# A ring of four weight slots, the low part written over the raw slot, and FFN loops unrolled by four

## What is computed

```python
def swiglu(h, w_gate, w_up, w_down):
    return (jax.nn.silu(h @ w_gate) * (h @ w_up)) @ w_down      # 1024 x 2816, 1024 x 2816, 2816 x 1024

x = x + 0.5 * swiglu(rms_norm(x, g[0]), ffn_w_gate[i, 0], ffn_w_up[i, 0], ffn_w_down[i, 0])
```

## Time and profile before

| | |
|---|---|
| median of 3 runs | 1438.19 us (1437.47 to 1438.66) |
| the profiled execution | 1436.46 us |
| its span (first to last instruction) | 1434.7 us |
| mean granted TensorE clock | 0.964 of full speed |
| HBM read | 231.58 MB |
| FFN stages on PE, first to last weight product | about 188 us each, five of them |

### The profile page before, as it was taken

One profiled execution on the slowest core, in us unless ns is written; L12 is line 12 of the kernel. 1 busy time (PEld: TensorE's weight loads), 2 busy tenths in 40 slices (PEclk: granted clock), 3 DMA queues, 4 the chain that ended last, 5 costly groups with the idle time before them and its releaser, 6 DMA issues.

```text
span 1434.7 us, 17436 instructions
## 1 busy us (share of the span) xinstructions
PE 1364.7 (95%) x6616; PEld 1129.3 (79%) x6616; DVE 794.6 (55%) x844; ACT 643.0 (45%) x722; POOL 72.0 (5%) x172
## 2 busy tenths in 40 slices
PE   6999998999999998999999899999998999999997
PEld 5888887867888876788887667888876986788885
DVE  4554469535545456554546755554556875555543
ACT  5434456324443435534345644434345543544342
POOL 2000012000000001000001200000001200000000
PEclk9999999889999999999999989999999996999999
DMA  8555544413655554455554303655553540466560
GB/s 257 192 188 179 201 162 141 153 59 118 206 191 189 183 215 151 145 178 197 183 188 135 117 30 118 221 189 179 201 198 118 170 171 30 138 202 199 179 198 37
DMA packets 158699, 233.29 MB, mean 163 GB/s; under 512 B 7496, under 2 KB 124894, under 8 KB 158654
## 3 DMA queue, kind: packets, MB, share of 16 engines
q1 hardware_dynamic: 156004, 229.19, 48.1%
q10 hardware_dynamic: 2170, 2.68, 0.6%
q0 software_dynamic: 480, 0.80, 0.3%
HBM read 231.58 MB, written 1.05 MB: 162 GB/s over the span
## 4 chain that ended last, share of the span: by engine, by line
PE 87%; DVE 7%; ACT 3%; DMA 1%; issue 1%; POOL 1%; SPq 0%; POOLq 0%; ACTq 0%; DVEq 0%
PE ps L230 25%; PE ps L232 25%; PE ps L231 25%; DVE wl L202 2%; PE ps L1117 2%; PE ps L469 2%; PE ps L311 1%; ACT wh L197 1%; PE ps L822 1%; DMA arena<-in_p 1%; PE ps L246 1%; PE ps L248 1%; PE ps L247 1%; DVE htl L344 1%; DVE x_rows L411 1%
## 5 line engine op out<-in xcount | busy, mean ns | idle before, releaser
L230 PE MATMUL ps<-wl,hth 128*128 128x512 f32 (+2 forms) x1274 | 506.8, 398 | 20.2 <-DVE htl L344 13.8
L232 PE MATMUL ps<-wh,htl 128*128 128x512 f32 (+2 forms) x1274 | 498.9, 392 | 0.0
L231 PE MATMUL ps<-wh,hth 128*128 128x512 f32 (+2 forms) x1274 | 498.7, 391 | 0.0
L600 DVE TENSOR_TENSOR wl<-raw,wh 128x2048 fp32r<-128x2048 f32 x120 | 275.1, 2293 | 204.8 <-ACT wh L556 204.8
L230 PEld LDWEIGHTS ps<-wl,hth 128*128 128x128 f32 x1274 | 243.5, 191 | 71.7 <-issue 13.9
L202 DVE TENSOR_TENSOR wl<-raw,wh 128x2048 fp32r<-128x2048 f32 (+2 forms) x99 | 222.1, 2256 | 139.6 <-ACT wh L197 139.6
L556 ACT ACTIVATE wh<-raw 128x2048 fp32r<-128x2048 f32 x120 | 229.6, 1914 | 123.7 <-PE ps L232 123.7
L232 PEld LDWEIGHTS ps<-wh,htl 128*128 128x128 f32 x1274 | 243.0, 191 | 51.1
L231 PEld LDWEIGHTS ps<-wh,hth 128*128 128x128 f32 x1274 | 243.8, 191 | 47.7
L197 ACT ACTIVATE wh<-raw 128x2048 fp32r<-128x2048 f32 (+2 forms) x99 | 184.3, 1871 | 100.6 <-PE ps L232 81.2
L230 PE MATMUL ps<-wl,prod_h 128*128 128x512 f32 x416 | 162.6, 391 | 0.0
(11 more groups left out here) (307 smaller groups left out, 938.1 us busy)
## 6 DMA issues: line engine op xcount, KB each, us to landing
raw<-in_ffn_w_gate SPq DMA_DIRECT2D x88, 512.0 KB, 4.0
raw<-in_ffn_w_up SPq DMA_DIRECT2D x88, 512.0 KB, 4.9
raw<-in_ffn_w_down SPq DMA_DIRECT2D x88, 512.0 KB, 3.9
raw<-in_w_gate_up SPq DMA_DIRECT2D x44, 512.0 KB, 4.7
raw<-in_even_w_in SPq DMA_DIRECT2D x24, 512.0 KB, 4.6
raw<-in_w_down SPq DMA_DIRECT2D x22, 512.0 KB, 3.9
raw<-in_ple_w_gate SPq DMA_DIRECT2D x16, 512.0 KB, 4.2
raw<-in_w_in SPq DMA_DIRECT2D x16, 512.0 KB, 4.5
```

Of the source, the lines that this page charges most:

```text
L230: nc.tensor.matmul(o, xh, b, start=first, stop=False)
L231: nc.tensor.matmul(o, xh, a, start=False, stop=False)
L232: return nc.tensor.matmul(o, xl, a, start=False, stop=last)
L600: nc.vector.tensor_tensor(wl[:, r, :], raw[:, r, :], wh[:, r, :].bitcast(f32), ALU.subtract)\
```

## The change

`raw` is allocated, given free at once, and `wl` is allocated in its place, so that both names stand for the same bytes: DVE writes the low part over the raw slot. The three rings have four buffers each. SP loads slot m once PE is done with slot m-4 (`weights_used`), where before it waited for the split of slot m-3. ACT's wait for PE ahead of a split becomes that for slot m-4. `Ahead.before` reaches one slot further, and the places in the FFN get `+ LEAD` (1), so every place now splits slot m+1 where it split slot m. The FFN loops have two iterations of four chunks on each of the four engines, with the first two chunks of SP's loop written out. `even_pe` waits for the DVE step `decayed` ahead of turning `e_last`, which no wait covered any longer.

The diff, cut to its core (DVE's and ACT's functions change in the same way):

```diff
-    RING = 3
+    RING = 4
+    LEAD = RING - 3
+    UNROLL = 4
...
-        raw = sb("raw", [P, RING, SLOT])
+        with nc.sbuf_tensor("raw", [P, RING, SLOT], f32) as raw:
+            pass
+        wl = sb("wl", [P, RING, SLOT], f32r)
         wh = sb("wh", [P, RING, SLOT], f32r)
-        wl = sb("wl", [P, RING, SLOT], f32r)
...
         def load_slot(sp, n, pieces):
             if n >= RING:
-                sp.wait_ge(split_ready, n - RING + 1)
+                sp.wait_ge(weights_used, n - RING + 1)
...
-            with sp.Fori(0, NCH - 1) as i:
+            for i in range(2):
                 for j in range(3):
...
+            with sp.Fori(0, (NCH - 3) // UNROLL) as it:
+                for i in range(2, 2 + UNROLL):
+                    for j in range(3):
+                        m = n + 2 + 3 * i + j
+                        sp.wait_ge(weights_used, it * (3 * UNROLL) + (m - RING + 1))
+                        pieces = gate_up(m, j, it * (UNROLL * HC) + (i + 1) * HC) if j < 2 else down(m, it * (2 * UNROLL) + 2 * i)
+                        for dst, src in pieces:
+                            sp.dma_start(dst, src).then_inc(raw_loaded[m % RING], 16)
...
-            with pe.Fori(2, NCH - 1) as c:
-                chunk(c, False)
+            with pe.Fori(0, (NCH - 3) // UNROLL) as it:
+                for c in range(2, 2 + UNROLL):
+                    chunk(it, c)
...
             norm_act(act, s, FFN_GAIN[f], FFN_BANKS)
-            act_ahead.through(act, n + 3)
+            act_ahead.through(act, n + 3 + LEAD)
             rms(act, s)
...
+            with act.Fori(0, (NCH - 3) // UNROLL) as it:
+                for c in range(2, 2 + UNROLL):
+                    split(it, n + 3 * c + 1 + LEAD)
+                    split(it, n + 3 * c + 2 + LEAD)
+                    silu(c, it=it)
+                    split(it, n + 3 * c + 3 + LEAD)
+                    high(c, it=it)
             act_ahead.n += 3 * (NCH - 3)
-            act_ahead.through(act, n + FFN_SLOTS - 1)
-            silu(n + 3 * (NCH - 1) + 1)
-            act_ahead.through(act, n + FFN_SLOTS)
+            act_ahead.through(act, n + FFN_SLOTS - 1 + LEAD)
+            silu(NCH - 1)
+            act_ahead.through(act, n + FFN_SLOTS + LEAD)
             high(NCH - 1, to=last_h)
...
             pe.wait_ge(EV_ACT.sem, EV_ACT.after("w_cols"))
+            pe.wait_ge(EV_DVE.sem, EV_DVE.after("decayed"))
```

More of the change, by code:

```diff
@@ L432, in ffn_load @@
                 load_slot(sp, n + j, gate_up(n + j, j, 0))
-            with sp.Fori(0, NCH - 1) as i:
+            for i in range(2):
                 for j in range(3):
[L436 to L439, removed]
+                    load_slot(sp, n + 2 + 3 * i + j, gate_up(n + 2 + 3 * i + j, j, i * HC + HC) if j < 2 else down(n + 4 + 3 * i, i * 2))
+            with sp.Fori(0, (NCH - 3) // UNROLL) as it:
[6 more added lines that the diff above has]
+                            sp.dma_start(dst, src).then_inc(raw_loaded[m % RING], 16)
             load_slot(sp, n + FFN_SLOTS - 1, down(n + FFN_SLOTS - 1, 2 * (NCH - 1)))
@@ L470, in turn_product, with chunk @@
                 m.then_inc(prod_turned, 1)
-            def chunk(c, first):
+            def chunk(it, c):
                 for half in range(2):
-                    pe.wait_ge(split_ready, c * 3 + (n + half))
+                    m = n + 3 * c - 1 + half
+                    pe.wait_ge(split_ready, it * (3 * UNROLL) + (m + 1))
                     for kk in range(4):
[L477 to L483, removed]
+                        gate_up(m, 4 * half + kk)
+                pe.wait_ge(prod_low, it * UNROLL + (c + f * NCH))
+                pe.wait_ge(split_ready, it * (3 * UNROLL) + (n + 3 * c + 2))
+                down(n + 3 * c + 1, False, False)
+                pe.wait_ge(prod_ready, it * UNROLL + (c + f * NCH + 1))
                 turn_product()
@@ L538, in ffn_act, with silu, high @@
         def ffn_act(act, n, s, f):
-            def silu(used, b=0):
-                act.wait_ge(weights_used, used)
+            def silu(c, b=0, it=0):
+                act.wait_ge(weights_used, it * (3 * UNROLL) + (n + 3 * c + (1 if c else 2)))
                 for tt in range(TT):
                     nc.scalar.activation(silu_g[:, tt, :], ps[:, b + tt, 0:HC], ACT.Silu, scale=rstd[:, tt:tt + 1]).then_inc(silu_ready, 1)
-            def high(c, b=2, to=prod_h):
-                act.wait_ge(prod_turned, c + (f * NCH + 1))
+            def high(c, b=2, to=prod_h, it=0):
+                act.wait_ge(prod_turned, it * UNROLL + (c + f * NCH + 1))
@@ L548, in high, with split @@
                 nc.scalar.activation(to[:, :, :], bank(b).rearrange("p (k t) -> p k t", k=2), ACT.Copy)\
                   .then_inc(prod_high, 1)
[L551 to L556, removed]
+            def split(it, m):
+                act.wait_ge(raw_loaded[m % RING], it * (32 * 3 * UNROLL // RING) + 32 * (m // RING + 1))
+                act.wait_ge(weights_used, it * (3 * UNROLL) + (m - RING + 1))
+                nc.scalar.activation(wh[:, m % RING, :], raw[:, m % RING, :], ACT.Copy).then_inc(high_ready, 1)
@@ L558, in ffn_act @@
             norm_act(act, s, FFN_GAIN[f], FFN_BANKS)
-            act_ahead.through(act, n + 3)
+            act_ahead.through(act, n + 3 + LEAD)
             rms(act, s)
-            silu(n + 2)
-            act_ahead.through(act, n + 4)
+            silu(0)
+            act_ahead.through(act, n + 4 + LEAD)
             high(0, 0)
-            act_ahead.through(act, n + 5)
-            silu(n + 4, 2)
-            act_ahead.through(act, n + 6)
+            act_ahead.through(act, n + 5 + LEAD)
+            silu(1, 2)
@@ L567, in ffn_act @@
+            act_ahead.through(act, n + 6 + LEAD)
             high(1)
[L568 to L573, removed]
+            with act.Fori(0, (NCH - 3) // UNROLL) as it:
[5 more added lines that the diff above has]
+                    high(c, it=it)
@@ L581, in ffn_dve, with multiply @@
         def ffn_dve(dve, n, s, f):
-            def multiply(c, b=0):
+            def multiply(c, b=0, it=0):
                 for tt in range(TT):
-                    dve.wait_ge(silu_ready, c * TT + (f * NCH * TT + tt + 1))
+                    dve.wait_ge(silu_ready, it * (TT * UNROLL) + (c * TT + f * NCH * TT + tt + 1))
                     m = nc.vector.scalar_tensor_tensor(out=prod[:, tt, :], in0=ps[:, b + tt, HC:2 * HC], scalar=rstd[:, tt:tt + 1],
@@ L588, in multiply, with low, split @@
                 m.then_inc(prod_ready, 1)
-            def low(c, b=2, to=prod_l, high=prod_h):
-                dve.wait_ge(prod_high, c + (f * NCH + 1))
+            def low(c, b=2, to=prod_l, high=prod_h, it=0):
+                dve.wait_ge(prod_high, it * UNROLL + (c + f * NCH + 1))
                 nc.vector.tensor_tensor(to[:, :, :], bank(b).rearrange("p (k t) -> p k t", k=2),
                                         high[:, :, :].bitcast(f32), ALU.subtract).then_inc(prod_low, 1)
[L596 to L600, removed]
+            def split(it, m):
+                dve.wait_ge(high_ready, it * (3 * UNROLL) + (m + 1))
+                nc.vector.tensor_tensor(wl[:, m % RING, :], raw[:, m % RING, :], wh[:, m % RING, :].bitcast(f32), ALU.subtract)\
@@ L601, in split @@
                   .then_inc(split_ready, 1)
             norm_dve(dve, s, FFN_GAIN[f], FFN_BANKS)
-            dve_ahead.through(dve, n + 3)
+            dve_ahead.through(dve, n + 3 + LEAD)
             multiply(0)
-            dve_ahead.through(dve, n + 4)
+            dve_ahead.through(dve, n + 4 + LEAD)
             low(0, 0)
-            dve_ahead.through(dve, n + 5)
+            dve_ahead.through(dve, n + 5 + LEAD)
             multiply(1, 2)
-            dve_ahead.through(dve, n + 6)
+            dve_ahead.through(dve, n + 6 + LEAD)
@@ L611, in ffn_dve @@
             low(1)
[L612 to L617, removed]
+            with dve.Fori(0, (NCH - 3) // UNROLL) as it:
+                for c in range(2, 2 + UNROLL):
+                    split(it, n + 3 * c + 1 + LEAD)
+                    split(it, n + 3 * c + 2 + LEAD)
+                    multiply(c, it=it)
+                    split(it, n + 3 * c + 3 + LEAD)
+                    low(c, it=it)
@@ L618, in ffn_dve @@
             dve_ahead.n += 3 * (NCH - 3)
-            dve_ahead.through(dve, n + FFN_SLOTS - 1)
+            dve_ahead.through(dve, n + FFN_SLOTS - 1 + LEAD)
             multiply(NCH - 1)
-            dve_ahead.through(dve, n + FFN_SLOTS)
+            dve_ahead.through(dve, n + FFN_SLOTS + LEAD)
             low(NCH - 1, to=last_l, high=last_h)
```

## The result

| | before | after |
|---|---|---|
| median, each of 6 runs | 1438.43 us (1437.24 to 1439.69) | 1515.75 us (1501.99 to 1532.49) |
| ratio after/before | | 1.051, 95% interval 1.0466 to 1.0554 |
| profiled execution, span | 1436.46, 1434.7 us | 1513.93, 1512.2 us |

What follows compares the result with a forecast made beforehand. PE bounds the kernel (busy 1364.7 of 1434.7 us), so only its waits or lower clock count. Terms 30 + 16.5 + 11 + 8.7 + 12 + 15 = 93 us on 1436.5 give 1529.5, forecast 1531 as median; range 1492 to 1562.

Steps and rivals of the forecast that it cites:

- The mechanism: At every split: load starts only at PE's release, when ACT's place wants it; split and work behind 5.6 us late.
- unrolling: Rival at the FFN loops' turns: instruction fetch, up to 45 us, partly hidden, 20 us taken: 1550; chance 0.1.
- the subtraction in place: DVE's subtraction with output over an input: 2.29 us either way, bounded by 0.1 us each way, hidden on DVE.
- FFN ends (7.5 each): Four FFNs with a stage behind: PE 2.4 late, then 4.2, then x adds late; stage ends 7.5 late, 30 us.
- Other ends (5.5 each): Ends of even, MLA, hybrid: x adds come one load later without slack, 5.5 us each, 16.5 us.
- PLEs (5.5): Both PLEs: last split stands ahead of ACT's table load and sigmoids, 5.5 us each, 11; DMA of p adds nothing.
- Inside the mixers (8.7): Late splits delay even's r_row (net 2.4 us), MLA's k chain (1.8) and hybrid's batch (about 4.5); together 8.7 us.
- Middle chunks (12 us): 8 chunks of 5 FFNs: multiply behind DVE's late split, PE 0.25 us late, 0.3 with semaphore hop; 12 us.
- The foreseen sign of it: Each FFN chunk: about 0.3 us of PE idle before the product's turn (L469) if the forecast is right.
- Clock (15 us): Stage ends, FFN ends, mixers: nine idle stretches bring PE to half clock, 1.7 us each, 15 us; bounds 0 to 30.
- the rest: Structure without middle chunks and clock: FFN ends 30, other ends 16.5, PLEs 11, mixers 8.7; 66 us.
- PE's busy time: Sign over the whole kernel: PE's busy time near 1375 us and its idle time near 150 if right.

Runs made afterwards that it cites:

- the unrolled kernel: Changed kernel with only the FFN loops' unrolling kept: raw has its own buffers, rings of three, loads wait for a split; 1436.92 us, ratio 1.0001 to the kernel before.
- The kernel with most unread matmuls: Changed kernel with places splitting as before the change, plus unread matmuls at PLE ends and in hybrid, even and MLA; 1422.14 us, ratio 0.9888 to the kernel before.

## Why the prediction was right, and where it was not

**The mechanism** (load and place hang on one event, and ACT's and DVE's other work queues behind the late split) is shown from both sides: taking away the tie alone removes all of the loss, and putting the places back group by group removes about what was expected of each group (44 us where 45 and some clock was expected, 22 where it was 16 to 22). The alternatives of unrolling and of the subtraction in place are out.

**FFN ends (7.5 each).** 7 to 9 us in three of them, and 13.9 in the fourth, with 2.4 foreseen for the chunks in each. In the fourth the issue of the last load came 1.6 us later than in the first, behind the half clock, and first issue to split took 6.2 us (1114.61 to 1120.80) where the first FFN's took 5.2. The DMA of p is issued behind that split and let PE go on only at 1127.40. The two ends of this FFN, before and after:

```profile
1068.71 2.55 DVE L411 SCALAR_TENSOR_TENSOR x_rows<-ps,x_rows 128x512 f32<-128x512 f32 x4
1071.50 0.66 PE L311 MATMUL ps<-ident,arena 128*128 128x128 f32 x4 [1.56 <-DMA arena<-in_p]
...
1124.95 2.48 DVE L414 SCALAR_TENSOR_TENSOR x_rows<-ps,x_rows 128x512 f32<-128x512 f32 x4
1127.40 1.12 PE L314 MATMUL ps<-ident,arena 128*128 128x128 f32 x4 [7.14 <-DMA arena<-in_p]
```

Before, PE already came for p 1.5 us after the first two adds (half of the four in the row), and now 1.2. So p slid with the rest, as foreseen, and added nothing of its own; what was too small is the lateness of the split ahead of it. The changed kernel's second profile shows nearly the same (14.1 us for the stage; 6.3 from issue to split; p 2.1 us after the first two adds, so at most 0.6 of its own).

**Other ends (5.5 each) and PLEs (5.5).** PE waits 5.75, 5.44 and 5.62 us for the adds where it waited 0.15, and the PLEs grew by 5.75 and 5.3 (6.9 and 6.4 in the second profile).

**Inside the mixers (8.7).** PE waits 3.50 us for r_row where it waited 0.52, and r_row itself is 3.0 later from the stage's start, where 3.4 was computed. With clock, even came out below (4.1 for 7.9), since it lost 8.5 us of work to half clock where it lost 11.5 before. Hybrid came out above in one profile (14.5 for 10) and far below in the other (3.5).

**Middle chunks (12 us): the step that failed.** "PE loads the product for turning at 80.08 ... So PE is 0.25 us late." 80.08 is the weight load's time, which runs ahead of the matmul. The two rows of the kernel before:

```profile
80.08 0.39 PE L232 MATMUL ps<-wh,prod_l 128*128 128x512 f32 x1
...
80.31 0.60 PE L469 MATMUL ps<-ident,prod 128*128 128x128 f32 x4
```

and the same chunk after:

```profile
80.95 0.39 PE L235 MATMUL ps<-wh,prod_l 128*128 128x512 f32 x1
81.14 0.42 PEld L477 LDWEIGHTS ps<-ident,prod 128*128 128x128 f32 x4 [0.22 <-DVE prod L597]
81.18 0.62 PE L477 MATMUL ps<-ident,prod 128*128 128x128 f32 x4
```

The weight load did wait 0.22 us, but the turn follows the last matmul by 0.23 us in both. A chunk takes 16.79 to 17.09 us in place of 16.81, together 3.8 us in 40 chunks (4.6 in the second profile), not 12. The foreseen sign of it, 0.3 us of PE idle before the turn in each chunk, is missing.

It was not that the transfers were faster: first issue to split was 5.42 us here, and the 512 KB DMAs of the up weights took 5.0 to land, as before. The Trainium skill's fit of DMA cost ("DMA: Bandwidth & Descriptors", the section on the anatomy of one DMA), an estimate of 4.4 us for 1 MB, does not agree with this 5.42; the page takes it from DMAs issued by GpSimd, and these are issued by SyncE.

**Clock (15 us).** 19.3 us of work lost in the profiled execution, 18.1 in the second, inside the bounds (0 to 30), but not where I put it: nine stretches of 1.7 us behind idle time. At the first FFN's end it was hidden by the late adds, and in the first profile 6.4 of the whole is the hybrid's attention (17.4 against 11.0), which I had not counted; the second profile has no such long stretch there. The rule behind the term does not hold either, as the same 2.52 us of idle time brought half clock in one trace and not in another. That this term came out near 15 is in good part luck, and against the 50.3 of the unrolled kernel it would be 9.

So terms of 4 for 12 and 19 for 15, with the rest at 54 for 66, make 77 for 93. The split between the last two is rough, since half clock that a late split hides counts as lost work and costs no time. Of what was to be seen, PE's busy time came to 1391 us and not near 1375, and its idle time to 121 and not near 150: less waiting, and more work at half clock, than foreseen.

## What to carry to other kernels

When a buffer is freed later, ask which place in the consumer's in-order stream hangs on the same event. If the load starts at the moment at which its consumer wants it, all of the load's time goes into everything queued behind that consumer, though the data itself is in time for PE; here one slot of distance between release and place gave back 77 us and kept the saved memory. For the margin of a wait on PE, read the matmul's row, not its weight load's. Where PE must wait anyway, matmuls into a free bank can keep its clock up; here they paid where no other late engine set the next step. And before a stage's added time is put down to the clock, a second profile of the same kernel should show it at the same place.

## What was not expected of the hardware

The runs of one kernel spread with their granted clock: the same program took 1501.99 us at 0.952 and 1532.49 at 0.933. The kernel with most unread matmuls had 0.983 to 0.988, and its six runs lay within 7 us. A weight load that waited 0.22 us cost the matmul behind it nothing (81.14 and 81.18 above).
